# The recurrence's dense key operand, copied by GpSimd instead of ScalarE

## The chip, the cores and the metric

The kernel runs on one core of a Trainium2 chip. The metric is the device time of one execution in microseconds (us), taken as the median of several runs. The engines go by short names: PE is TensorE, DVE is VectorE, ACT is ScalarE, POOL is GpSimd and SP is SyncE, which issues most DMAs.

## The reference, cut to what matters

The reference runs 512 tokens of 1024 features through two blocks. The first has two layers, each with two gated feed-forward parts and a mixer (differential attention in layer 0, spatial gating in layer 1). The second block has one layer with a gated linear recurrence, an output projection and a squared-ReLU feed-forward part. The change lies in the recurrence of the second block alone:

```python
def _hgrn2_chunk_scan(q, k, v, log_f):
    """S_t = diag(f_t) S_{t-1} + k_t v_t^T ; o_t = S_t^T q_t.  All (B,S,H,X) float32."""
    ...
        cum = jnp.cumsum(gi, axis=2)
        ...
        scores = jnp.einsum('bhtk,bhtsk,bhsk->bhts', qi, decay, ki)
        o_intra = jnp.einsum('bhts,bhsv->bhtv', scores, vi)
```

There are 8 heads of 128 features. q, k, v, the forget gate f and an output gate g come from one projection of the normalised input (`hgrn_w_in_2`, 1024 x 4096), and the result goes through `hgrn_w_out_2`.

## The kernel before, in words

Every weight matrix is streamed in tiles of 1024 x 256 (16 for the recurrence's projection). SP loads a tile into `w_raw`; ACT rounds it to `w_hi_t` (L981, two halves); the remainder `w_lo_t` is the difference of the two. Each product is then three matmuls: high by high, high by low, low by high. The remainders are computed by POOL (L809), except for 16 tiles, numbers `rest0` to `rest0 + 15`, which are those that run during the recurrence: there DVE does it in four quarters of a tile (L1311, the steps "rest"). POOL's loop skips those tiles, so in the original kernel it has nothing to do in that stretch.

The recurrence treats the heads in four stages j of two heads each. It does not scan over chunks: it builds the decayed score matrix of 512 x 512 per head by doubling. At level s, with h = 2^s, blocks of 2h tokens are split in an early and a late half; the late half's queries meet the early half's keys, both already scaled by the gates' products. `hgrn_sequence()` writes one order of steps for all engines by hand, and each engine walks through the same list and does its own share of it: "gemm" steps (half a unit of the projection, 12 matmuls, to fill PE), "lev" steps (slots 0 to 9 of a stage), "far", "out", "osum", "hn" and "lo" for what follows, and "conv", "rest" and "prep" for weights and gates. Each engine's queue is in order, and the engines meet by semaphores.

One level goes round like this. When PE has finished the matmuls of the slot before (semaphore `hg_mm`), DVE does `update`: it multiplies the early keys by the gates (L1281, called `k_early`, which raises `hg_kk`), then the late queries (L1282, called `q_late`, which raises `hg_qk`), then a product of gates that shrinks with the level (L1286, from 512 columns down to 8). Keys and gates are `hg_k`, `hg_q` and `hg_f`, all parts of the SBUF tensor `scr`. Then `keep` takes the scores of the level before out of the bank by a masked copy (L1303, COPY_PREDICATED, mask in SBUF, data in a PSUM bank). Quarters of weight remainders (L1311), gate preparations (L1318, L1319) and pieces of the output (L1333 to L1342) stand between the levels in DVE's queue.

PE's matmuls of a level (L1837) need the early keys as a dense operand of 128 columns, while they lie in `hg_k` in runs of h columns in two halves of the sequence. `early_keys` makes the dense copy `hg_both`, 128 x 512, level by level, 7 levels in 4 stages. ACT does it when `hg_kk` says that `k_early` is done, and raises `hg_km`; for level 0 of the next stage it does so in the step "out" of the stage before. PE waits for `hg_qk`, `hg_km` and `hg_pc` (the masked copy two levels back), does the level, and goes on with one or two "gemm" fills. Slots 8 and 9 (L1843, L1852) need no dense copy.

Of the kernel before, what the change touches and what calls it, by code (L numbers as in the profile page):

```python
# [16 lines left out]
S = 512  # L17
# [14 lines left out]
LEVELS = 7  # L32
# [334 lines left out]
def build_program(nc, ins, out):  # L367
    ops, T = make_plan()
    with ExitStack() as ctx:
# [3 lines left out]
        def sem(name):  # L373
            return ctx.enter_context(nc.semaphore(name))
# [92 lines left out]
        hg_k = scr[:, 4096:6144].rearrange("p (b t) -> p b t", b=2)  # L467
        hg_q = scr[:, 6144:8192].rearrange("p (b t) -> p b t", b=2)
        hg_mask = scr[:, 8192:8192 + LEVELS * S].rearrange("p (l a n t) -> p l a n t", l=LEVELS, a=2, n=4)
        hg_both = scr[:, 11776:11776 + S]  # L470
# [81 lines left out]
        hg_in = sem("hg_in")  # L552
        hg_qk = sem("hg_qk")
        hg_kk = sem("hg_kk")
        hg_km = sem("hg_km")
        hg_mm = sem("hg_mm")
# [22 lines left out]
        def blk(t, n):  # L579

            return t[:, bass.ds(n * S, S)] if not isinstance(n, int) else t[:, n * S:(n + 1) * S]

        def bcast(ap, dims):

            return bass.AP(tensor=ap.tensor, offset=ap.offset, ap=[list(ap.ap[0])] + dims)


        def turned(ap):

            return bass.AP(tensor=ap.tensor, offset=ap.offset + P - 1, ap=[list(ap.ap[0]), [P, 2], [-1, P]])  # L590
# [10 lines left out]
        def hg_cols(t, j, b):  # L601

            return t[:, j % 2, :].rearrange("p (u b t) -> p u b t", u=2, b=2)[:, :, b, :]
# [25 lines left out]
        rest0 = next(op.t0 for op in ops if op.kind == "hgrn") + 2  # L629

        def on_dve(t):

            return rest0 <= t < rest0 + HG_RESTS
# [7 lines left out]
        def half_rows(t, hf):  # L641

            return slice(4, tile_kb[t]) if hf else slice(0, 4)
# [157 lines left out]

        @block.gpsimd
        def _(pool):

            for t in range(n_tiles):
                for hf in range(0 if on_dve(t) else 2):
                    k = half_rows(t, hf)
                    pool.wait_ge(w_hi, 2 * t + hf + 1)
                    nc.gpsimd.tensor_tensor(w_lo_t[:, t % 2, k], w_raw[:, t % 2, k], w_hi_t[:, t % 2, k].bitcast(F32),  # L809
                                            ALU.subtract).then_inc(w_lo, 1)  # L810
# [75 lines left out]
        def hgrn_act(act, op, conv, inverse_root):  # L886
            def unit_out(u):
                kind, j = HG_TILES[u // 2]
                b, bank = u % 2, ps[u if u < 4 else u % 2]
                halves = bank[:].rearrange("p (u t) -> p u t", u=2)  # L890
                act.wait_ge(blk_mm, 2 * op.t0 + u + 1)
                if kind in "fq" and j >= 2:
                    act.wait_ge(hg_mm, 10 * (j - 1))
                if kind == "v" and j:
                    act.wait_ge(o_mm, 8 + 2 * j)
                if kind == "g" and j:
                    act.wait_ge(o_ok, 8 + 2 * j)
                if kind == "f":
                    act.activation(hg_cols(hg_f, j, b), halves, ACT.Sigmoid)
                    act.activation(hg_cols(hg_k, j, b), halves, ACT.Sigmoid, scale=-1.0).then_inc(hg_ev, 1)  # L900
                elif kind == "q":
                    act.activation(hg_cols(hg_q, j, b), halves, ACT.Silu).then_inc(hg_ev, 1)
                elif kind == "v":
                    act.activation(hg_v[:, 2 * b:2 * b + 2, :], bank[:].rearrange("p (t n) -> p t n", t=2), ACT.Copy,
                                   scale=H_SCALE).then_inc(hg_ev, 1)
                else:
                    act.activation(hg_g[:, b, :], bank[:], ACT.Silu).then_inc(hg_ev, 1)

            def early_keys(j, s):

                h = 1 << s
                act.copy(hg_both.rearrange("p (n a h) -> p n a h", a=2, h=h),
                         bcast(hg_k[:, j % 2, 0:1], [[2 * h, S // (2 * h)], [S + h, 2], [1, h]])).then_inc(hg_km, 1)

            for step in hgrn_sequence():
                if step[0] == "first":
                    unit_out(0)
                    unit_out(1)
                elif step[0] == "gemm" and step[2] == 1:
                    unit_out(step[1])  # L920
                elif step[0] == "conv":
                    t = op.t0 + step[1] + 2
                    conv(t % 2, t)
                elif step[0] == "lev" and step[2] < LEVELS:
                    _, j, s = step
                    if s:
                        act.wait_ge(hg_kk, 8 * j + s)
                        early_keys(j, s)
                    elif j == 0:
                        act.wait_ge(hg_in, 2)  # L930
                        early_keys(j, s)
                elif step[0] == "far":
                    _, j, k = step
                    act.wait_ge(hg_mm, 10 * j + 9 + k)
                    if k == 0:
                        src = ps[4][:].rearrange("p (b c t) -> p b c t", b=2, c=2)
                        dst = bcast(hg_far_p[:, 0:P], [[2 * HG_FAR, 2], [4 * HG_FAR, 2], [1, P]])
                        act.activation(dst, src, ACT.Copy).then_inc(hg_far, 1)
                    else:
                        for b in range(2):  # L940
                            src = ps[5 - b][:].rearrange("p (c t) -> p c t", c=2)
                            dst = bcast(hg_far_p[:, 2 * b * HG_FAR + P:2 * b * HG_FAR + S - P],
                                        [[HG_FAR - P, 2], [1, 2 * P]])
                            act.activation(dst, src, ACT.Copy).then_inc(hg_far, 1)
                elif step[0] == "out":
                    _, j, b = step
                    if j < 3 and b == 0:
                        act.wait_ge(hg_in, 2 * j + 4)
                        act.wait_ge(hg_mm, 10 * j + LEVELS + 1)
                        early_keys(j + 1, 0)  # L950
                    act.wait_ge(o_mm, 8 + 2 * j + b + 1)
                    if j:
                        act.wait_ge(a_lo_s, op.a0 + 2 * (j - 1) + b + 1)
                    act.activation(sq[:, b, :], ps[6 - b][:], ACT.Square).then_inc(o_sq, 1)
                elif step[0] == "osum":
                    j = step[1]
                    act.preload_act_table_set("natural_log_exp_and_others")
                    for b in range(2):
                        act.wait_ge(o_ss, 8 + 2 * j + b + 1)
                        if j:  # L960
                            act.wait_ge(o_ok, 8 + 2 * (j - 1) + b + 1)
                        inverse_root((rstd, ssq)[b][:], ps[7 if b == 0 else 4][:], eps, 1.0 / P, o_root)
                elif step[0] == "hn":
                    _, j, b = step
                    act.wait_ge(o_ok, 8 + 2 * j + b + 1)
                    hd = 2 * j + b
                    act.copy(blk(a_hi_t, hd)[:, 0:HS], sq[:, b, 0:HS])
                    act.copy(blk(a_hi_t, hd)[:, HS:S].rearrange("p (u t) -> p u t", u=2), turned(sq[:, b, HS:S]))\
                       .then_inc(a_hi_s, 1)
# [1307 lines left out]
```

## Time and profile before

| what | before |
| --- | --- |
| median of 3 runs | 2604.66 us (2604.43 to 2604.9) |
| the profiled execution | 2604.72 us |
| its span (first to last instruction) | 2602.9 us |
| mean granted TensorE clock | 0.995 |
| the stretch that the change touches | about 1960 to 2200 us |

The rows further below are copied from the profile. A row of a group of instructions names the line of the kernel, the engine, the operation, what is written and read with the shape, and how often; times are microseconds unless marked ns. Where tensors share one allocation the name is that of the allocation (`scr`, `hidden`, `bank`). In rows in order of time the first number is the start from the span's start, the second the time to the end of the last of the merged instructions, and a bracket at the end gives the idle time of the engine just before and who ended it. Idle time of an engine other than PE costs nothing by itself.

### The profile page before, as it was taken

How to read it: one execution, taken by the hardware profiler on the slowest of the kernel's cores; microseconds unless marked ns; L12 is line 12 of the kernel's file. 1: busy time of each engine (PE TensorE's matmuls, PEld its weight loads, DVE VectorE, ACT ScalarE, POOL GpSimd, SP SyncE). 2: the span in 40 equal slices, each digit the busy share in tenths (PEclk: the TensorE clock that was granted, in tenths of full speed). 3: DMA queues.
4: the chain of work that ended last, by engine and by line, in shares of the span. 5: the costliest groups of instructions: out<-in, count | busy, mean ns of one | idle time of the engine just before them, and what ended most of it. 6: DMA issues, size and time to landing. Idle time of an engine off the chain costs nothing.

```text
span 2602.9 us, 30201 instructions
## 1 busy us (share of the span) xinstructions
PE 2554.0 (98%) x12530; PEld 2121.7 (82%) x12530; DVE 1093.0 (42%) x1542; ACT 910.6 (35%) x1395; POOL 997.3 (38%) x404
## 2 busy tenths in 40 slices
PE   5999999999999999999999999999999999999999
PEld 4888888776888888888888988888888888888887
DVE  6726254445532325854445255211156555512213
ACT  3222225555422223422224333222254444423324
POOL 1445444221444444444444444444430000444442
PEclk8999999999999999999999999999999999999999
DMA  8545343111333343545452323323222221333231
GB/s 287 200 164 195 118 157 128 63 64 49 114 130 129 130 138 106 202 154 186 138 190 86 115 81 130 115 96 126 93 87 87 71 69 49 96 99 97 93 97 71
DMA packets 249215, 312.13 MB, mean 120 GB/s; under 512 B 7357, under 2 KB 227150, under 8 KB 248951
## 3 DMA queue, kind: packets, MB, share of 16 engines
q1 hardware_dynamic: 246762, 308.88, 35.8%
q8 instruction: 99, 1.62, 0.3%
q10 hardware_dynamic: 2316, 1.33, 0.2%
q14 instruction: 38, 0.30, 0.0%
HBM read 308.07 MB, written 4.74 MB: 120 GB/s over the span
## 4 chain that ended last, share of the span: by engine, by line
PE 94%; DVE 3%; issue 1%; ACT 1%; POOL 0%; DVEq 0%; ACTq 0%
PE bank L1917 21%; PE bank L1912 21%; PE bank L1913 20%; PE bank L1929 5%; PE bank L1930 5%; PE bank L1934 5%; PE bank L1895 2%; PE bank L1896 2%; PE bank L1897 2%; PE bank L1944 1%; PE bank L1945 1%; PE bank L1946 1%; PE bank L1751 1%; PE bank L1837 1%; PE bank L1771 1%
## 5 line engine op out<-in xcount | busy, mean ns | idle before, releaser
L809 POOL TENSOR_TENSOR w_lo_t<-w_raw,w_hi_t 128x1024 fp32r<-128x1024 f32 (+1 forms) x400 | 997.1, 2512 | 1580.6 <-ACT w_hi_t L981 1580.2
L981 ACT CAST w_hi_t<-w_raw 128x1024 fp32r<-128x1024 f32 (+1 forms) x432 | 424.9, 1032 | 696.2 <-PE bank L1917 576.4
L1912 PE MATMUL bank<-h_hi,w_hi_t 128*128 128x512 f32 x1648 | 642.1, 390 | 0.0
L1913 PE MATMUL bank<-h_lo,w_hi_t 128*128 128x512 f32 x1648 | 641.2, 389 | 0.0
L1917 PE MATMUL bank<-h_hi,w_lo_t 128*128 128x512 f32 x1648 | 415.2, 391 | 0.0
L1912 PEld LDWEIGHTS bank<-h_hi,w_hi_t 128*128 128x128 f32 x1648 | 309.3, 188 | 64.3 <-issue 0.5
L1913 PEld LDWEIGHTS bank<-h_lo,w_hi_t 128*128 128x128 f32 x1648 | 309.4, 188 | 64.2 <-issue 0.2
L1917 PEld LDWEIGHTS bank<-h_hi,w_lo_t 128*128 128x128 f32 x1648 | 309.3, 188 | 64.0
L1430 DVE SCALAR_TENSOR_TENSOR scr<-scr,cact 128x1024 f32<-128x1024 f32 x112 | 253.4, 2262 | 76.3 <-DMA scr<-in_ada_w 68.2
L1912 PE MATMUL bank<-act_hi,w_hi_t 128*128 128x512 f32 x720 | 280.3, 389 | 0.3 <-DVE x L1632 0.2
L1913 PE MATMUL bank<-act_lo,w_hi_t 128*128 128x512 f32 x720 | 280.1, 389 | 0.0
L1607 DVE TENSOR_TENSOR bank<-hidden,bank 128x512 f32<-128x512 f32 x88 | 61.1, 694 | 438.2 <-ACT hidden L1142 438.2
L1632 DVE SCALAR_TENSOR_TENSOR x<-bank,half,x 128x512 f32<-128x512 f32 x88 | 66.1, 751 | 338.1 <-PE bank L1917 260.9
L1142 ACT ACTIVATE hidden<-bank 128x512 f32<-128x512 f32 x88 | 52.6, 598 | 368.6 <-PE bank L1917 368.6
L1917 PE MATMUL bank<-act_hi,w_lo_t 128*128 128x512 f32 x720 | 178.7, 389 | 0.1
L1912 PEld LDWEIGHTS bank<-act_hi,w_hi_t 128*128 128x128 f32 x720 | 135.1, 188 | 29.2 <-DVE x L1632 0.6
L1917 PEld LDWEIGHTS bank<-act_hi,w_lo_t 128*128 128x128 f32 x720 | 135.1, 188 | 28.5 <-POOL w_lo_t L809 0.5
L1913 PEld LDWEIGHTS bank<-act_lo,w_hi_t 128*128 128x128 f32 x720 | 135.2, 188 | 28.1
L1929 PE MATMUL bank<-act_hi,w_hi_t 128*128 128x512 f32 x320 | 128.1, 400 | 0.1
L1930 PE MATMUL bank<-act_lo,w_hi_t 128*128 128x512 f32 x320 | 124.7, 390 | 0.0
L1929 PE MATMUL bank<-h_hi,w_hi_t 128*128 128x512 f32 x288 | 121.1, 421 | 0.0
L1934 PE MATMUL bank<-act_hi,w_lo_t 128*128 128x512 f32 x320 | 114.3, 390 | 0.0
(267 smaller groups left out, 3335.5 us busy)
## 6 DMA issues: line engine op xcount, KB each, us to landing
scr<-in_ada_w SPq DMA_DIRECT2D x128, 512.0 KB, 6.7
w_raw<-in_ffn_wg SPq DMA_DIRECT2D x44, 1024.0 KB, 5.4
w_raw<-in_ffn_wu SPq DMA_DIRECT2D x44, 1024.0 KB, 5.4
w_raw<-in_ffn_wd SPq DMA_DIRECT2D x32, 1024.0 KB, 5.0
w_raw<-in_mlp_w SPq DMA_DIRECT2D x32, 1024.0 KB, 5.3
w_raw<-in_hgrn_w_in SPq DMA_DIRECT2D x16, 1024.0 KB, 5.5
w_raw<-in_ffn_wd SPq DMA_DIRECT2D x16, 768.0 KB, 4.3
w_raw<-in_attn_w_qkv SPq DMA_DIRECT2D x12, 1024.0 KB, 5.1
```

Source lines behind the costliest of these rows:

```text
L809: nc.gpsimd.tensor_tensor(w_lo_t[:, t % 2, k], w_raw[:, t % 2, k], w_hi_t[:, t % 2, k].bitcast(F32), ALU.subtract).then_inc(w_lo, 1)
L981: act.copy(w_hi_t[:, slot, k], w_raw[:, slot, k]).then_inc(w_hi, 1)
L1142: act.activation(blk(hidden, 4 + (2 * i + b) % 4), ps[b][:], ACT.Silu).then_inc(act1, 1)
L1430: dve.scalar_tensor_tensor(acc, src, cact[:, kb:kb + 1], acc, ALU.mult, ALU.add).then_inc(ada_ch, 1)
L1607: dve.tensor_tensor(ps[2 + b][:], blk(hidden, 4 + (2 * i + b) % 4), ps[2 + b][:], ALU.mult).then_inc(v_done, 1)
L1632: ins_ = dve.scalar_tensor_tensor(xb, acc[:], gate_col(op, nb), xb, ALU.mult, ALU.add)
L1912: pe.matmul(dst, w, blk(m_hi, kb), start=kb == 0, stop=False)
L1913: pe.matmul(dst, w, blk(m_lo, kb), start=False, stop=False)
L1917: last = pe.matmul(dst, w_lo_t[:, slot, kb, b * P:(b + 1) * P], blk(m_hi, kb), start=False, stop=kb == kbs - 1)
L1929: pe.matmul(dst, w, blk(m_hi, kb), start=kb == 0, stop=False)
L1930: pe.matmul(dst, w, blk(m_lo, kb), start=False, stop=False)
L1934: last = pe.matmul(dst, w_lo_t[:, slot, kb, b * P:(b + 1) * P], blk(m_hi, kb), start=False, stop=kb == kbs - 1)
```

## The change

The 28 copies of `early_keys` move from ACT's queue to POOL's. On POOL they stand in a loop of their own over the four stages and seven levels, ahead of the loop's turn for tile `rest0`, with the same semaphores: level 0 of a stage waits for that stage's gate preparations and for the last dense level of the stage before, the others wait for `k_early`. Source, destination, shape and what PE waits for are unchanged. ACT's steps "lev" are left without work, and its step "out" loses the copy for the next stage.

```diff
         @block.gpsimd
         def _(pool):
+            def early_keys(j, s):
+
+                h = 1 << s
+                nc.gpsimd.tensor_copy(hg_both.rearrange("p (n a h) -> p n a h", a=2, h=h),
+                                      bcast(hg_k[:, j % 2, 0:1], [[2 * h, S // (2 * h)], [S + h, 2], [1, h]]))\
+                    .then_inc(hg_km, 1)
 
             for t in range(n_tiles):
+                if t == rest0:
+                    for j in range(4):
+                        for s in range(LEVELS):
+                            if s == 0:
+                                pool.wait_ge(hg_in, 2 * j + 2)
+                                if j:
+                                    pool.wait_ge(hg_mm, 10 * (j - 1) + LEVELS + 1)
+                            else:
+                                pool.wait_ge(hg_kk, 8 * j + s)
+                            early_keys(j, s)
...
-            def early_keys(j, s):
-
-                h = 1 << s
-                act.copy(hg_both.rearrange("p (n a h) -> p n a h", a=2, h=h),
-                         bcast(hg_k[:, j % 2, 0:1], [[2 * h, S // (2 * h)], [S + h, 2], [1, h]])).then_inc(hg_km, 1)
-
...
-                elif step[0] == "lev" and step[2] < LEVELS:
-                    _, j, s = step
-                    if s:
-                        act.wait_ge(hg_kk, 8 * j + s)
-                        early_keys(j, s)
-                    elif j == 0:
-                        act.wait_ge(hg_in, 2)
-                        early_keys(j, s)
...
-                    if j < 3 and b == 0:
-                        act.wait_ge(hg_in, 2 * j + 4)
-                        act.wait_ge(hg_mm, 10 * j + LEVELS + 1)
-                        early_keys(j + 1, 0)
```

## Rows read from the trace of the kernel before

**Rows 1.** The page: busy time by engine; the chain that ended last, by engine.
```profile
PE 2554.0 (98%) x12530; PEld 2121.7 (82%) x12530; DVE 1093.0 (42%) x1542; ACT 910.6 (35%) x1395; POOL 997.3 (38%) x404
...
PE 94%; DVE 3%; issue 1%; ACT 1%; POOL 0%; DVEq 0%; ACTq 0%
```

**Rows 2.** Windows: stretch, length, busy PE, PEld, DVE, ACT, POOL; clock; DMA.
```profile
2030.00:2094.00 64.00, 61.62 (x362) 53.39 (x361) 37.32 (x62) 28.08 (x42) 0.00 (x0) 1.00 0.23 66
2094.00:2158.00 64.00, 61.62 (x362) 53.38 (x361) 37.30 (x62) 28.07 (x42) 0.00 (x0) 1.00 0.22 67
```

**Rows 3.** Line L912, the copies on ACT: ns minimum/median/maximum, first and last start.
```profile
L912 ACT COPY scr<-scr x28: 618/624/877, 1965.5 to 2181.9; 128x512 f32<-128x512 f32 x28
```

**Rows 4.** Waits from 1955 to 2215: us in total, times, longest.
```profile
ACT scr L912 <- DVE scr L1281: 46.9, 23, 4.1
...
PEld bank L1837 <- DVE scr L1282: 6.4, 4, 2.1
```

**Rows 5.** POOL's first instruction after the recurrence, in order of time.
```profile
2216.12 2.40 POOL L809 TENSOR_TENSOR w_lo_t<-w_raw,w_hi_t 128x1024 fp32r<-128x1024 f32 x1 [265.53 <-ACT w_hi_t L981]
```

**Rows 6.** Line L809, POOL's subtractions, both shapes.
```profile
L809 POOL TENSOR_TENSOR w_lo_t<-w_raw,w_hi_t x400: 1286/2395/3943, 40.3 to 2575.7; 128x1024 fp32r<-128x1024 f32 x129, 128x512 fp32r<-128x512 f32 x5
```

**Rows 7.** Lines L1430 and L1632, two DVE instructions.
```profile
L1430 DVE SCALAR_TENSOR_TENSOR scr<-scr,cact x112: 1264/2204/3485, 59.5 to 1643.0; 128x1024 f32<-128x1024 f32 x112
...
L1632 DVE SCALAR_TENSOR_TENSOR x<-bank,half,x x88: 750/751/752, 149.7 to 1926.1; 128x512 f32<-128x512 f32 x88
```

**Rows 8.** DVE and POOL around 185 us, in order of time.
```profile
184.34 1.27 DVE L1430 SCALAR_TENSOR_TENSOR scr<-scr,cact 128x1024 f32<-128x1024 f32 x1
...
184.81 3.07 POOL L809 TENSOR_TENSOR w_lo_t<-w_raw,w_hi_t 128x1024 fp32r<-128x1024 f32 x1 [6.14 <-ACT w_hi_t L981]
185.72 3.23 DVE L1430 SCALAR_TENSOR_TENSOR scr<-scr,cact 128x1024 f32<-128x1024 f32 x1
```

**Rows 9.** DVE in the second stage: the starts K2 to K7, and what follows K3.
```profile
2031.79 0.69 DVE L1281 TENSOR_TENSOR scr<-scr 128x512 f32<-128x512 f32 x1 [0.61 <-PE bank L1837]
...
2036.41 0.69 DVE L1281 TENSOR_TENSOR scr<-scr 128x512 f32<-128x512 f32 x1
2037.01 0.69 DVE L1282 TENSOR_TENSOR scr<-scr 128x512 f32<-128x512 f32 x1
2037.74 0.62 DVE L1286 TENSOR_TENSOR scr<-scr 128x256 f32<-128x256 f32 x1
...
2040.35 0.68 DVE L1281 TENSOR_TENSOR scr<-scr 128x512 f32<-128x512 f32 x1
...
2043.17 0.69 DVE L1281 TENSOR_TENSOR scr<-scr 128x512 f32<-128x512 f32 x1 [0.34 <-PE bank L1837]
...
2047.58 0.68 DVE L1281 TENSOR_TENSOR scr<-scr 128x512 f32<-128x512 f32 x1
...
2053.37 0.69 DVE L1281 TENSOR_TENSOR scr<-scr 128x512 f32<-128x512 f32 x1
```

**Rows 10.** PE's level matmuls in the same stage: T2, T3, T4, T6, T7.
```profile
2034.46 0.51 PE L1837 MATMUL bank<-scr 128*128 128x128 f32 x3
...
2038.24 0.61 PE L1837 MATMUL bank<-scr 128*128 128x128 f32 x4
...
2042.01 0.61 PE L1837 MATMUL bank<-scr 128*128 128x128 f32 x4
...
2049.29 0.60 PE L1837 MATMUL bank<-scr 128*128 128x128 f32 x4
...
2054.81 0.57 PE L1837 MATMUL bank<-scr 128*128 128x128 f32 x3 [1.74 <-DVE scr L1282]
```

**Rows 11.** First stage, K6; fourth stage, K7 and T7.
```profile
1984.61 0.69 DVE L1281 TENSOR_TENSOR scr<-scr 128x512 f32<-128x512 f32 x1 [0.47 <-PE bank L1837]
...
2180.53 0.69 DVE L1281 TENSOR_TENSOR scr<-scr 128x512 f32<-128x512 f32 x1
...
2182.59 0.91 PE L1837 MATMUL bank<-scr 128*128 128x128 f32 x6 [1.50 <-DVE scr L1282]
```

## The prediction

> **What bounds the kernel now.** I read the page first, then the recurrence's stretch by windows, its waits, and one stage of it in order of time. TensorE (PE) is busy 98% of the span and makes 94% of the chain that ended last [rows 1]. So whatever PE waits is lost for good, and work moved between the other engines counts only where it makes PE wait longer or shorter. The change touches one stretch, from about 1960 to 2200 us, with GpSimd (POOL) entirely idle, VectorE (DVE) busy 37 of 64 us and ScalarE (ACT) 28 of 64 in a middle stage, at a granted clock of 1.00 [rows 2].
>
> In that stretch each level s of a head pair runs round a loop: PE's level matmuls, then on DVE `k_early` (L1281), `q_late` (L1282), a small product (L1286), the masked copy (L1303) and parts of the weight rests (L1311); ACT copies the key operand (L912) when `k_early` is done, beside `q_late`; PE starts the next level when both are there. The 28 ACT copies cost 618 to 877 ns [rows 3]. ACT waits for `k_early` 46.9 us in all, but nothing waits for ACT's copy: PE's weight loads wait for `q_late` (6.4 us at L1837) [rows 4]. So there is little to win from a quicker copy, and the question is what the new place of the copy does to DVE and thus to PE.
>
> **The change, part by part.** *Removed from ACT:* 28 copies, some 18 us by their median, and its waits. As PE waits for none of them, I count 0. What ACT does next is to evict PE's banks and convert weights, and there it waits for PE. Should this free something, PE's 6.4 us at L1837 [rows 4] are the ceiling; since that wait is on DVE, I keep 0.
>
> *Added to POOL:* 28 copies with their waits, ahead of its loop's later weight tiles. Behind them stands only the tile that POOL starts at 2216.12 after 265.53 us idle [rows 5], later than the last copy can be, so nobody waits there; SP's weight loads in the stretch count DVE's rests, not POOL. No DMA is moved.
>
> *What one copy lasts on POOL, d.* No row shows it. Nearest above: POOL's own two-input subtraction, 1.286 us at its least (the 128x512 form) and 2.395 at the median (128x1024) [rows 6], so 2.17 ns a column and 0.18 fixed. Nearest below: ACT's 0.62 for the same copy [rows 3]. A copy reads one stream where the subtraction reads two; half the slope gives 0.18 + 0.56 = 0.74. But the source jumps between two halves in runs of 2^s columns, and ACT's 877 against 618 says that short runs cost. I take 0.9 us and keep 0.62 and 1.29 as ends. POOL offers no reason for less than ACT's time; below it lies only the case that the copy costs PE nothing, a rival below.
>
> The Trainium skill speaks on d from both sides: "GPSIMD Engine Reference", section Engine selection, calls one-input work roughly line rate (an estimate at 1.2 GHz: 0.43 us plus the fixed part, about the lower end), while its section Performance pitfalls for Q7 kernels puts reads with a step above 8 bytes at about 2.9 cycles an element (an estimate of 1.24 us, about the upper end). No row here shows either for a copy; by the first the sum below would be about +13, by the second about +28.
>
> *Who holds the port.* This decides the sign. L1430 on DVE reads two tensors in SBUF and lasts 1264 ns at its least but 3485 at most; L1632 reads one from SBUF and one from a bank and stays at 750 to 752 in all 88 [rows 7]. In one place in order of time: the first L1430 runs 184.34 to 185.61 undisturbed; POOL's subtraction, started at 184.81, needs 3.07 and ends at 187.88, that is 2.27 after DVE let go; the next L1430 starts at 185.72, lasts 3.23, and so ends 1.07 after POOL [rows 8]. They take turns, each for a whole instruction, and one that waits gets in before the other engine's next.
>
> In the recurrence `k_early`, `q_late`, L1286 and L1311 all read two tensors in SBUF; L1303 reads its data from a bank. `q_late` is issued straight behind `k_early`, so when `k_early` releases POOL, `q_late` has the port: the copy starts after `q_late`, not beside it. Then L1286 waits for the copy to end. So a level is hit twice: the copy arrives d after `q_late` instead of with it, and DVE loses d.
>
> *The sum for one stage.* Call K2 to K7 the starts of `k_early` and T2 to T7 those of PE's level matmuls. In the old trace T7 stands 1.44 after K7 (1.29 for both products, 0.15 to the matmul). The new rules, with 0.01 more for the second release: T ≥ K + 1.45 + d; T ≥ old T plus PE's shift so far; the next K = old K (less DVE's idle before it) plus DVE's shift plus d, and at least T + 1.16. With d = 0.9 and the second stage [rows 9, 10]:
>
> K2 follows PE, 2031.79, so T2 ≥ 2034.14, under its 2034.46: shift 0. K3 = 2036.41 + 0.9 = 2037.31, T3 = 2039.66 (old 2038.24): +1.42. K4 = 2040.35 + 1.8 = 2042.15, T4 = 2044.50 (2042.01): +2.49. K5 has 0.34 idle ahead, so the greater of 2045.53 and T4 + 1.16 = 2045.66; T5 stays at +2.49. K6 = 2047.58 + 2.49 + 0.9 = 2050.97, T6 = 2053.32 (2049.29): +4.03. K7 = 2053.37 + 3.39 + 0.9 = 2057.66, T7 = 2060.01 (2054.81): +5.2, in which PE's old wait of 1.74 is contained and so not counted twice. After T7 no copy is needed until the next stage, whose copy of level 0 has several us of room.
>
> The third stage repeats the second 64.0 us later, with the same busy times [rows 2]: +5.2. In the first, DVE has 0.47 more idle ahead of K6: +4.7. In the fourth, K7 stands 0.84 nearer and T7 0.24 nearer than in the second: 5.2 - 0.84 + 0.24 = +4.6 [rows 11]. Sum 4.7 + 5.2 + 5.2 + 4.6 = 19.7 us. With d = 0.62 the same steps give 3.0 + 3.5 + 3.5 + 2.9 = 12.9; with 1.29, 7.0 + 7.5 + 7.5 + 6.9 = 28.9.
>
> The profiled execution took 2604.72 us, its span 2602.9; the runs' median is 2604.66, 0.06 away. So 2604.7 + 19.7 = 2624.4.
>
> **The rivals.**
> *A, the copy stays beside `q_late`:* the turn-taking of [rows 8] is between two instructions that each read two tensors, and a copy reads one. If it needs nothing that `q_late` uses, DVE keeps its times and PE can start at K + 0.69 (`k_early` alone) + d + 0.2 (0.15 to the matmul as above, the rest for the release, an estimate). At 0.9 that is K + 1.79: late by 0.13 at T4, 0.08 at T6 and 0.35 at T7, some 0.4 a stage and under 2 in all, 2606.5; with 1.29 still only about +3. It decides from the first level on: not slower beyond what can be told. For it: the different kind of instruction. Against it: DVE's side of the conflict is the same, and POOL's copy reads SBUF too.
> *B, ACT's relief reaches PE:* ACT evicts and converts up to a copy and its wait earlier, DVE's preparations and rests follow sooner and PE's waits for `q_late` shrink. At the very most 6.4 us, 2598.3; against it, DVE is idle ahead of only K2 and K5 in the second stage, so it is not ACT that makes it late [rows 9].
> *C, the copy is far slower than 1.29* because of the broken runs. From 1.29 on every level is bound by DVE or the copy, and the slope between the two ends above is 24 us per us of d; at d = 2 that is 28.9 + 17 = 46, 2651.
>
> **How the numbers follow.** A measurement of this kernel tells about 0.2%, 5.2 us, from no change. My forecast (taking turns, d from 0.62 to 1.29, 2617.6 to 2633.6) gets 0.76, C 0.10, A 0.10, B 0.04. All of the forecast and C is slower: 0.86; A is within 0.2%; B is called faster whole, 0.04. The range: 2610 to 2638. Below lie A and B; above, most of C; between 2610 and 2617 I hold some of the forecast, for a copy shorter than ACT's or an L1286 that gets in first.
>
> **What would show it.** Right: POOL's new copies are recorded longer than they need, starting just after `k_early` and ending 0.6 us plus d later; L1286 lasts its old time plus up to d; L1281 and L1282 stay near 0.69; PE's waits at L1837 rise by about 20 us and now end on POOL; the stages are some 5 us longer each. The step of the port is wrong if copies end before `q_late` and L1286 keeps its times (A). The size is wrong if the levels with short runs last above 1.3. The forecast is wrong altogether if PE's waits don't grow.

## The result, and the profile after

The changed kernel takes 2614.55 us (median of 6 runs, 2612.87 to 2615.73) against 2604.43 before: 10.1 us more, a ratio of 1.0038 with a 95% interval of 1.0027 to 1.0049. It is slower, as forecast, by half of what was forecast. The profiled execution is the quickest of the six, 2612.87 us, 8.15 over the one before.

The page of the changed kernel: busy time by engine; the chain that ended last; POOL's copies (line engine op, count, busy us, mean ns, idle before and who ended it).
```profile
PE 2558.8 (98%) x12530; PEld 2123.0 (81%) x12530; DVE 1102.3 (42%) x1542; ACT 893.0 (34%) x1367; POOL 1030.0 (39%) x432
...
PE 93%; DVE 3%; issue 1%; ACT 1%; POOL 0%; DVEq 0%; ACTq 0%
...
L807 POOL COPY scr<-scr 128x512 f32<-128x512 f32 x28 | 32.5, 1162 | 208.1 <-DVE scr L1279 179.2
```
ACT is 17.6 us less busy, POOL 32.7 more (its copies are 32.5) and DVE 9.3 more, though DVE has the same 1542 instructions as in [rows 1]. PE has 4.8 us more busy time with the same matmuls: 2.4 of it lies in the second stage, where the clock falls for a while (below); each of the other three has some 0.7 more, whose cause was not looked for.

The level that stands as K3 in [rows 9], in the changed kernel, DVE and POOL in order of time (L1279, L1280, L1284, L1301 are the old L1281, L1282, L1286, L1303).
```profile
2037.19 0.69 DVE L1279 TENSOR_TENSOR scr<-scr 128x512 f32<-128x512 f32 x1
2037.79 0.69 DVE L1280 TENSOR_TENSOR scr<-scr 128x512 f32<-128x512 f32 x1
2037.94 1.01 POOL L807 COPY scr<-scr 128x512 f32<-128x512 f32 x1 [3.91 <-DVE scr L1279]
2038.51 0.91 DVE L1284 TENSOR_TENSOR scr<-scr 128x256 f32<-128x256 f32 x1
2039.46 1.32 DVE L1301 COPY_PREDICATED hidden<-scr,bank 128x512 f32<-128x512 int32 x1
```
The copy starts 0.06 us behind `k_early`, is recorded for 1.01 and ends at 2038.95, 0.47 after `q_late` (2038.48). The small product lasts 0.91 where it lasted 0.62. So the copy trails `q_late` and pushes DVE, but by 0.47 and 0.29, not by 0.9 and 0.9.

PE's level matmuls T2 to T7 of the second stage, after; they answer to [rows 10].
```profile
2034.88 0.51 PE L1835 MATMUL bank<-scr 128*128 128x128 f32 x3
...
2039.05 0.57 PE L1835 MATMUL bank<-scr 128*128 128x128 f32 x3 [0.23 <-issue]
...
2043.29 0.57 PE L1835 MATMUL bank<-scr 128*128 128x128 f32 x3 [0.23 <-issue]
...
2047.01 0.49 PE L1835 MATMUL bank<-scr 128*128 128x128 f32 x3
...
2051.06 0.57 PE L1835 MATMUL bank<-scr 128*128 128x128 f32 x3 [0.27 <-issue]
...
2057.15 0.91 PE L1835 MATMUL bank<-scr 128*128 128x128 f32 x6 [2.19 <-DVE scr L1280]
```
T2 stands 0.42 later than before (the shift that the stage begins with). From there T3, T4, T6 and T7 are 0.81, 1.28, 1.77 and 2.34 later, so this stage's levels add 0.39, 0.86, 1.35 and 1.92. The profile puts these waits on "issue" or on `q_late`, but what came last is the copy. The two rows before T7:
```profile
2055.89 0.68 DVE L1280 TENSOR_TENSOR scr<-scr 128x512 f32<-128x512 f32 x1
...
2056.03 1.01 POOL L807 COPY scr<-scr 128x512 f32<-128x512 f32 x1 [5.07 <-DVE scr L1279]
```
`q_late` ended at 2056.57, the copy at 2057.04, and PE began 0.11 after it.

PE right after T7, in the second stage and in the third.
```profile
2057.15 1.27 PE L1835 MATMUL bank<-scr 128*128 128x128 f32 x8 [2.19 <-DVE scr L1280]
2058.07 0.77 PE L1927 MATMUL bank<-h_hi,w_hi_t 128*128 128x512 f32 x1
2058.64 0.63 PE L1928 MATMUL bank<-h_lo,w_hi_t 128*128 128x512 f32 x1
2059.07 0.63 PE L1927 MATMUL bank<-h_hi,w_hi_t 128*128 128x512 f32 x1
...
2124.68 1.13 PE L1835 MATMUL bank<-scr 128*128 128x128 f32 x8 [2.19 <-DVE scr L1280]
...
2125.88 0.40 PE L1928 MATMUL bank<-h_lo,w_hi_t 128*128 128x512 f32 x1
2126.11 0.40 PE L1927 MATMUL bank<-h_hi,w_hi_t 128*128 128x512 f32 x1
```
In the second stage the matmuls that follow the idle time start 0.43 apart (2058.64 to 2059.07); in the third they start 0.23 apart. Windows of this kernel (length; busy PE, PEld, DVE, ACT, POOL; granted clock; DMA) say why:
```profile
2054.50:2058.00 3.50, 1.31 (x10) 0.92 (x9) 3.40 (x8) 0.00 (x0) 1.01 (x1) 1.00 0.00 0
2058.00:2061.00 3.00, 3.00 (x10) 2.42 (x9) 1.91 (x5) 0.00 (x0) 0.00 (x0) 0.50 0.18 40
2061.00:2064.00 3.00, 3.00 (x13) 2.43 (x13) 0.21 (x1) 1.33 (x3) 0.00 (x0) 0.93 0.96 306
```
The granted clock is 0.50, the level of 1.2 GHz, after PE had been busy 1.31 of 3.50 us. ACT's eviction, which follows that fill, and with it slot 8 come 1.6 us later. In the third stage the same idle time of 2.19 was followed by no such stretch.

The profiled execution adds up so: levels 1.4 + 1.9 + 1.9 + 1.3 = 6.5 us by the shifts of T2 to T7 in the four stages; 1.6 for the half clock; 0.7 at slot 8 of the third stage, where the level 0 copy cut in ahead of `q_late` (L1280 lasted 1.34 there, 0.69 elsewhere). That is 8.8. The stretch began 0.9 earlier than in the kernel before (its first level at 1967.64 for 1968.55); a lead of that size is there already near 436 us, where an idle time of PE ends at 435.64 for 436.60, far ahead of anything that was changed. Together they make the difference of the spans, 7.8, to 0.1.

### The profile page after: what moved, and what is told of

Same layout as the page of the kernel before. It is cut to its first block, busy times and chain, and to the rows that moved or that the text cites. A ratio compares the mean times of both kernels' runs of the same rounds, so it can differ in the third digit from the quotient of the medians.

```text
span 2610.7 us, 30201 instructions
## 1 busy us (share of the span) xinstructions
PE 2558.8 (98%) x12530; PEld 2123.0 (81%) x12530; DVE 1102.3 (42%) x1542; ACT 893.0 (34%) x1367; POOL 1030.0 (39%) x432
## 3 DMA queue, kind: packets, MB, share of 16 engines
q10 hardware_dynamic: 2316, 1.33, 0.2%
## 4 chain that ended last, share of the span: by engine, by line
PE 93%; DVE 3%; issue 1%; ACT 1%; POOL 0%; DVEq 0%; ACTq 0%
PE bank L1915 21%; PE bank L1910 20%; PE bank L1911 20%; PE bank L1927 5%; PE bank L1928 5%; PE bank L1932 5%; PE bank L1893 2%; PE bank L1894 2%; PE bank L1895 2%; PE bank L1942 1%; PE bank L1943 1%; PE bank L1944 1%; PE bank L1835 1%; PE bank L1749 1%; PE bank L1769 1%
## 5 line engine op out<-in xcount | busy, mean ns | idle before, releaser
L1915 PE MATMUL bank<-act_hi,w_lo_t 128*128 128x512 f32 x720 | 178.8, 389 | 0.1
L807 POOL COPY scr<-scr 128x512 f32<-128x512 f32 x28 | 32.5, 1162 | 208.1 <-DVE scr L1279 179.2
```

The costliest lines, as they stand in the source:

```text
L1915: last = pe.matmul(dst, w_lo_t[:, slot, kb, b * P:(b + 1) * P], blk(m_hi, kb), start=False, stop=kb == kbs - 1)
```

## The experiments

Theory 1: POOL and DVE take turns, as the prediction said, but a copy is short: alone some 0.6, of which 0.5 trails `q_late`. Theory 2: no turns; the copy simply needs the recorded 1.0 us. Theory 3: the cost is in ACT's changed order or in the level 0 copies.

**The gate operand from a bank.** The same edit was made to both kernels, so that DVE's three products of a level read one tensor from SBUF and one from a PSUM bank. It leaves out the gates' product: DVE compares with what lies in the bank, so the outcome is another, while the work has the same shape.
```diff
-                dve.tensor_tensor(k_early, k_early, spots(F, *up, one), ALU.mult).then_inc(hg_kk, 1)
-                dve.tensor_tensor(q_late, q_late, spots(F, *low, one), ALU.mult).then_inc(hg_qk, 1)
+                gate = bcast(ps[6][:, 0:1], [[HS, 2], [h, n], [1, h]])
+                dve.tensor_tensor(k_early, k_early, gate, ALU.is_ge).then_inc(hg_kk, 1)
+                dve.tensor_tensor(q_late, q_late, gate, ALU.is_ge).then_inc(hg_qk, 1)
...
-                    link(dve.tensor_tensor(ups, ups, spots(F, *low, []), ALU.mult))
+                    link(dve.tensor_tensor(ups, ups, bcast(ps[6][:, 0:1], [[HS, 2], [1, n]]), ALU.is_ge))
```


> The changed kernel, but k_early, q_late and the small gate product take their second operand from PSUM bank 6 instead of hg_f in SBUF, and compare with it instead of multiplying (the scores are another thing; the work is of the same shape). Theory 1, turn-taking: with one SBUF operand left on DVE, POOL's copy starts about 0.08 us behind k_early, lasts about 0.5 us at levels 1 to 6 (about 0.7 at level 0) and ends before q_late; q_late and the small product are not lengthened; the time is within 2 us of the same edit with the copies on ACT, run beside it. Theory 2, the copy simply needs 1.0 us on POOL: it is still recorded at about 1.0 and ends about 0.4 us after q_late; 1 to 4 us over the ACT version. Theory 3, the cost lies elsewhere (ACT's changed order, level 0): still 8 to 10 us over the ACT version.

> The kernel before with the same edit of the gate operand (from a PSUM bank, compared instead of multiplied). It is the base for the run above. All theories: within 4 us of the kernel before, for k_early and q_late keep 512 columns each; the ACT copies stay at 0.62 us.

With the copies on POOL 2603.57 us, with the copies on ACT 2604.29, the kernel before 2604.43 beside them: POOL's copies cost nothing that can be told once the products read one SBUF tensor. The copies of this run over all levels (ns minimum/median/maximum), and the same level as above, in order of time:
```profile
L807 POOL COPY scr<-scr x28: 614/616/3047, 1958.4 to 2180.2; 128x512 f32<-128x512 f32 x28
...
2035.42 0.68 DVE L1280 TENSOR_TENSOR scr<-scr,bank 128x512 f32<-128x512 f32 x1
2036.02 0.68 DVE L1281 TENSOR_TENSOR scr<-scr,bank 128x512 f32<-128x512 f32 x1
2036.17 0.62 POOL L807 COPY scr<-scr 128x512 f32<-128x512 f32 x1 [3.93 <-DVE scr L1280]
2036.74 0.64 DVE L1285 TENSOR_TENSOR scr<-scr,bank 128x256 f32<-128x256 f32 x1
```
The copy starts at the same point, takes 0.62 and is over at 2036.79, just after `q_late` (2036.70); the small product keeps 0.64. Theory 2 falls: 1.01 is 0.62 plus a wait. Of the wait of 0.54 (2037.94 to 2038.48) some 0.15 are not lost: 0.47 follow `q_late`, not 0.62. Theory 3 falls too, as ACT's queue is the changed one here and level 0 is on POOL. At level 0, in runs of one column, the copies of the last three stages took 0.86 in this run, at level 1 0.68. The 3047 is the first copy of all: it meets four instructions L1310, which still read two SBUF tensors (more on it below).

**Level 0 alone, and levels 1 to 6 alone on POOL.** Both edits are to the kernel before; only POOL's loops are shown, ACT loses the copies that move.
```diff
 b_dense0
+                    for j in range(4):
+                        pool.wait_ge(hg_in, 2 * j + 2)
+                        if j:
+                            pool.wait_ge(hg_mm, 10 * (j - 1) + LEVELS + 1)
+                        early_keys(j, 0)
 c_levels
+                    for j in range(4):
+                        for s in range(1, LEVELS):
+                            pool.wait_ge(hg_kk, 8 * j + s)
+                            early_keys(j, s)
```


> Only the four copies of level 0 are on POOL, the others stay on ACT. Theory 1: no level waits for them, so 0 to +2 us, the +2 where a copy cuts in between k_early and q_late of slot 8 of the stage before (about 0.6 us each, at most 3 times). Theory 3, that the level 0 copies carry the cost: +4 us or more. Theory 2: 0.

> Only the copies of levels 1 to 6 are on POOL, level 0 stays on ACT. Theory 1 and theory 2: the levels' share, +6.5 us, and up to +10 where PE's long wait before the last level is followed by a stretch at half the granted clock (1.6 us each time). Theory 3: under +3.

Level 0 alone: 2605.87, +1.4, ratio 1.0005 (0.9996 to 1.0014), not told from no change. Levels 1 to 6 alone: 2612.49, +8.1, ratio 1.0033 (1.002 to 1.0045). Its trace has the same steps per level as the changed kernel, 6.4 us together, and one stretch at half clock (1.6 us) after T7 of the second stage, none after T7 of the third, though PE had idled 2.21 and 2.20 us there. Levels 1 to 6 carry the cost. The two parts sum to 9.5 of the 10.1.

**Each copy of levels 1 to 6 made twice.**
```diff
+                if s:
+                    if j or s > 1:
+                        pool.wait_ge(hg_x, 6 * j + s - 1)
+                    nc.gpsimd.tensor_copy(spare[:].rearrange("p (n a h) -> p n a h", a=2, h=h), ...)\
+                        .then_inc(hg_x, 1)
```


> The changed kernel with each copy of levels 1 to 6 made twice on POOL, first into a spare tensor that nobody reads and then into the operand. Theory 1 (turn-taking; a copy alone is 0.62 us, of which 0.5 follow q_late, and VectorE's small product loses 0.33): the prediction's recurrence with these sizes gives 3.5 us a stage if the small product gets in between the two copies, 5 if it does not: +14 to +20 over the kernel before, and 2 to 5 more where TensorE's longer waits before the last level are followed by half the clock. Were the levels' room larger than the recurrence says, it would stay near +10 to +12.

2618.15 us, +13.9, ratio 1.0055 (1.0041 to 1.0069), just at the low end of theory 1's range. POOL and DVE of this run in order of time:
```profile
2044.38 0.68 DVE L1288 TENSOR_TENSOR scr<-scr 128x512 f32<-128x512 f32 x1
2044.52 1.01 POOL L812 COPY spare<-scr 128x512 f32<-128x512 f32 x1 [2.24 <-DVE scr L1287]
...
2045.10 0.70 DVE L1292 TENSOR_TENSOR scr<-scr 128x128 f32<-128x128 f32 x1
...
2045.48 0.79 POOL L815 COPY scr<-scr 128x512 f32<-128x512 f32 x1
```
The small product gets in between the two copies: it ends at 2045.80, and the second copy 0.47 later, again 0.47. By the shifts of T the four stages lost 16.7 us in the profiled execution (2620.81 us, the slowest of its four runs). Two stretches at half clock after T7, each with 2.2 us of idle PE ahead, make 3.2 of them. At slot 8 of three stages the level 0 copy got in ahead of `q_late` (L1288 lasted 1.33 to 1.35), which makes 1.9. The levels themselves lost 2.7, 3.2, 3.2 and 2.5, 11.6 together: less than the 3.5 a stage, 14 in all, that was expected of them.

**One fill moved ahead of the last dense level,** on both kernels.
```diff
-HG_FILLS = (1, 1, 1, 1, 1, 1, 1, 2, 2, 2, 2, 1)
+HG_FILLS = (1, 1, 1, 1, 1, 1, 2, 2, 2, 2, 1, 1)
```


> The kernel before with one fill of the projection moved from slot 10 of a stage to slot 6, in the first three stages. TensorE's wait of 1.74 us before the last dense level in stages 2 and 3 is filled: -2 to -3.5 us. If the wait only moves (to slot 8, or to the outputs, which then have one fill fewer before them), 0 or slower.

> The changed kernel with the same move of one fill. It takes away TensorE's idle time of 2.2 us before the last dense level, after which 3.4 us at half the granted clock were seen in stage 2. If that idle time is what the clock falls after: no such stretch, and 4 to 7 us less than the changed kernel, +3 to +6 over the kernel before. If the clock has another cause, the half-clock stretch stays and the gain is 2 to 3.5 us as in the run above.

On the kernel before: 2598.41, -5.8, ratio 0.9978 (0.9969 to 0.9986), more than expected, since slot 8's waits of 0.64 went too. On the changed kernel: 2604.95, 9.6 less than the changed kernel's median and level with the kernel before (1.0003, 0.9994 to 1.0012), also more than expected. No stretch at half clock is left in these stages; the window that had it:
```profile
2058.00:2061.00 3.00, 3.00 (x18) 2.62 (x19) 2.96 (x7) 2.98 (x4) 0.67 (x1) 1.00 0.94 302
```
The two kernels with this fill order differ by 6.5 us over 11 runs each. By the shifts of T in their two traces, neither of which has a stretch at half clock, the levels cost 6.0 (0.9, 1.9, 1.9 and 1.3): the first stage costs 0.4 less in this order.

**The gate preparations on ScalarE.**
```diff
-                    dve.tensor_scalar(F, F, one_lb[:, hd:hd + 1], lb[:, hd:hd + 1], ALU.mult, ALU.add)
-                    dve.tensor_scalar(K, K, one_lb[:, hd:hd + 1], None, ALU.mult).then_inc(hg_in, 1)
+                    act.activation(hg_cols(hg_f, j, b), hg_cols(hg_f, j, b), ACT.Identity,
+                                   bias=lb[:, hd:hd + 1], scale=one_lb[:, hd:hd + 1])
+                    act.activation(hg_cols(hg_k, j, b), hg_cols(hg_k, j, b), ACT.Copy,
+                                   scale=one_lb[:, hd:hd + 1]).then_inc(hg_in, 1)
```


> The kernel before with the gate preparations (two instructions per unit, 8 units) on ScalarE instead of VectorE. If VectorE's load is what makes TensorE wait in this stretch, its waits before the last dense level lose 0.86 us in two stages and the waits before slot 8 (0.64 in three stages) go: -2 to -4 us. If the waits have another cause: 0.

2603.53, -0.7, ratio 0.9997 (0.9988 to 1.0006). The levels did gain, 0.75 at T7 in two stages and 0.8 to 0.9 at slot 8 in three, but ACT's longer eviction delayed the first level 0: PE idled 2.9 us there (0.8 before) and then ran 3.4 us at half clock, 1.5 us lost after it. As a version it is a miss, -2 to -4 being expected; the shorter waits do show that DVE's load sets PE's waits here.

**Two tries to go further,** on the kernel before: the fill moved in the fourth stage too, and then the preparations of stages 2 to 4 on ACT.
```diff
-            counts = (1, 1, 1, 1, 1, 1, 1, 1, 2, 2, 2, 0)
+            counts = (1, 1, 1, 1, 1, 1, 2, 1, 2, 2, 1, 0)
```


> A version meant to beat both: the copies on ScalarE as before, one fill moved from slot 10 to slot 6 in all four stages. In the first three stages this measured -5.8 us; in the fourth TensorE still waited 1.5 to 1.9 us before the last dense level. If that wait is filled as well: -7 to -7.7 us, 2596.5 to 2597.4. If the fourth stage's last outputs then wait instead, no more than -5.8.

> The run above with the gate preparations of stages 2 to 4 on ScalarE too (the first stage's stay on VectorE, where ScalarE had delayed the first level by 1.5 us). VectorE is freed of 0.86 us per unit; with the fill moved, the residual wait before the last dense level is some 0.6 us in two stages: -1 us against the run above. If VectorE is no longer what TensorE waits for there: 0.

2598.73 and 2599.03 (ratios 0.9978 and 0.9979): no further gain, the poorer of the two outcomes expected of each. In the fourth stage T7 took its fill, but slots 8 and 9 then waited for `q_late` (0.38 and 0.19 us of idle PE), and with the preparations on ACT no wait of PE became shorter. The quickest kernel of the study is the one before with one fill moved, 2598.4, which the two tries match within what can be told.

## Why the prediction was right in kind and wrong in size

*What bounds the kernel: right.* Only what made PE wait counted. ACT's relief of 17.6 us brought next to nothing, as said: with the copies on POOL and no turns to take, the gain was 0.7 us (the bank runs), not told from none; their traces show rival B in one place alone, T7 of the fourth stage, where PE idled 0.86 instead of 1.46.

*Who holds the port: right for levels 1 to 6, and shown.* The copy trails `q_late`, L1284 gets longer, L1279 and L1280 stay at 0.69, and all of it goes when the products read one SBUF tensor. Rival A is thereby out for this kernel; it is just what the bank runs make of it.

*Who comes next: wrong as a rule.* The prediction read from [rows 8] that the engine that waits gets in before the other's next instruction. Three level 0 copies of the changed kernel, with the DVE instructions around them:
```profile
1958.35 2.49 DVE L1309 TENSOR_TENSOR w_lo_t<-w_raw,w_hi_t 128x512 fp32r<-128x512 f32 x4
1958.50 3.05 POOL L807 COPY scr<-scr 128x512 f32<-128x512 f32 x1 [8.83 <-DVE scr L1317]
...
1997.26 1.84 POOL L807 COPY scr<-scr 128x512 f32<-128x512 f32 x1 [6.14 <-DVE scr L1317]
1997.72 0.69 DVE L1280 TENSOR_TENSOR scr<-scr 128x512 f32<-128x512 f32 x1
...
2130.74 1.25 POOL L807 COPY scr<-scr 128x512 f32<-128x512 f32 x1 [6.17 <-DVE scr L1317]
2131.20 1.34 DVE L1280 TENSOR_TENSOR scr<-scr 128x512 f32<-128x512 f32 x1
```
The first waits for all four of DVE's instructions and ends 0.71 after the last; the second starts during `k_early` and waits for `q_late` too, ending 0.69 after it; the third, at the same point of a later stage, gets in between the two. So a copy can lose its turn to a row of DVE instructions that follow each other at once, and which way it goes was not the same in the same place. In the levels it made no difference: each of those 24 copies was recorded at 1.01 to 1.07, behind `q_late` and ahead of the small product.

*What one copy lasts on POOL: the step that failed.* I put d at 0.9, between POOL's halved subtraction (0.74) and the whole one (1.29), for the sake of the short runs. Alone it is 0.62, ACT's own time and the lower end; the prediction's own sum for 0.62 is 12.9 in place of 19.7. The short runs cost as they do on ACT: 0.86, 0.68, 0.62 at levels 0, 1 and above, against ACT's 0.88, 0.69 and 0.62, and of the two longer ones only level 1 stands in a round of the loop, where T2 did not move. Of the two estimates from the Trainium skill ("GPSIMD Engine Reference") the one from Engine selection, line rate, agrees with the 0.62; the one for wide steps from Performance pitfalls for Q7 kernels, 1.24, is not borne out even at level 0.

*The same step, a second time:* I let the whole d follow `q_late` and the whole d fall on DVE. The first rows had shown otherwise: a POOL subtraction that lasts 2.40 at the median [rows 6] ended 2.27 after DVE had let go, and a DVE instruction of 1.27 ended 1.07 after POOL [rows 8]. About 0.1 to 0.2 of each hides behind the wait; I take it for start-up, which no trace shows. For a long subtraction this is nothing; for a copy of 0.62 it leaves 0.47 at PE, and 0.29 to 0.35 on DVE. This takes the sum from 12.9 to the 6.5 that the levels measured, so the two errors in d weigh about the same.

*The recurrence: right in form.* With 0.47 and 0.29 in place of 0.9 and 0.9 its rules for the second stage give shifts of 0.38, 0.84, 0.84, 1.34 and 1.90 at T3 to T7; measured were 0.39, 0.86, 0.93, 1.35 and 1.92. The two sizes are from the same trace, so this tests the form alone. Four stages measure 6.5 instead of 19.7. For the doubled copies, where the sizes were set before the run, it gave 3.5 a stage and 2.5 to 3.2 were measured.

*What I left out:* the clock. Its price follows PE's idle time before T7, which the change raised from 1.74 to 2.19; 1.6 us each time it falls. And I gave the level 0 copy "several us of room": it has that at PE, but in one stage it got in ahead of `q_late` of slot 8, for 0.7 us.

*What would show it:* PE's waits did not rise by 20 us, and the profile does not name POOL in them. The stages became 1.3 to 3.5 us longer, not 5.

*Luck in the range:* the median lies inside 2610 to 2638, but the room that I kept below 2617 was for a copy shorter than ACT's or for an L1286 that gets in first. Neither happened; the levels' 6.5 alone would give 2611, and the rest comes from terms that I had left out and from what is still open below.

*Still open:* the profiled execution accounts for 8.8 us in the stretch, while the medians differ by 10.1. The half clock came once in two equal idle times in the changed kernel and in the run of levels 1 to 6 alone, and twice in the run with doubled copies, so its count may differ between executions; there is one profile of each kernel, and that it does was not shown. Level 0 alone measured +1.4 us, while its profiled execution shows no wait longer than before.

## What to carry to other kernels

Where DVE reads two tensors in SBUF, a copy moved to POOL doesn't run beside it but after it, at times after a whole row of such instructions, and holds up DVE's next one; count it on both sides, but count only the part that is left behind the wait. The same copy's time on ACT was the better bound for an unseen one-input copy on POOL here, not POOL's two-input work. And where PE waits at one point of a hand-written order, look first for a fill to move there: this gave 5.8 us, where the move of the copies could have given 0.7 at most.

## What the runs showed of the hardware that I had not expected

A 128x512 f32 copy on POOL took 0.62 us, as on ACT, while POOL's subtraction of the same shape takes 1.29. After 2.16 to 2.9 us of idle PE the granted clock was at 0.50 for 3.4 us in five places (changed kernel, levels 1 to 6 alone, doubled copies twice, preparations on ACT), and stayed at 1.00 in two others after 2.19 and 2.20 (changed kernel, levels 1 to 6 alone); it stayed at 1.00 after the 1.74 of the kernel before. A POOL copy that waits for DVE's two-input instructions waited for one, two, three or four of them in a row (1.25, 1.84 and 3.05 us recorded in the changed kernel and 2.46 with the fill moved, for a level 0 copy of 0.86 alone).
